# Layer openings of a two-layer diffusion backbone: the first two FFN tiles by token halves, with the splits moved between engines

## What is computed

```python
hx = modulate(rms_norm(x, norm1_g[l]), sh1x, sc1x)        # h * (1 + scale) + shift
x = x + g1x * mixer(hx)
x = x + g2x * swiglu(modulate(rms_norm(x, norm2_g[l]), sh2x, sc2x), ffn_w1[l], ffn_w3[l], ffn_w2[l])
def swiglu(h, w1, w3, w2):
    return (jax.nn.silu(h @ w1) * (h @ w3)) @ w2
```

## Time and profile before

| | us |
|---|---|
| median of three runs | 1555.65 (1554.92 to 1555.9) |
| the profiled execution | 1555.58 |
| its span, first to last instruction | 1553.8 |
| TensorE busy | 1489.6 (96%) |
| VectorE, ScalarE, GpSimd busy | 998.7, 699.8, 661.8 |

### The profile page before, as it was taken

How to read it: one execution, slowest core, us unless ns; L and a number is a source line. 1 busy time by engine, 2 the same in 40 slices (tenths; PEclk the granted TensorE clock), 3 DMA queues, 4 the chain that set the end, 5 groups by cost and what they waited for, 6 DMA issues and landing times.

```text
span 1553.8 us, 26593 instructions
## 1 busy us (share of the span) xinstructions
PE 1489.6 (96%) x10378; PEld 1271.7 (82%) x10378; DVE 998.7 (64%) x1480; ACT 699.8 (45%) x1211; POOL 661.8 (43%) x449
## 2 busy tenths in 40 slices
PE   6999999899899999999999999999999999999997
PEld 3888864479798889999899998855568998998997
DVE  5898877669586867667475455767623655455465
ACT  4745335562733324324243544245537354444355
POOL 0031036412655425444344333355646665556462
PEclk9999999999999999999999999999999999999999
DMA  9632110054124333354343111200012324224222
GB/s 376 217 117 80 43 42 0 3 199 152 58 99 159 109 119 127 116 181 154 120 159 113 61 63 55 68 28 1 1 55 70 129 77 134 70 93 131 89 95 82
DMA packets 51676, 157.07 MB, mean 101 GB/s; under 512 B 5568, under 2 KB 13120, under 8 KB 50016
## 3 DMA queue, kind: packets, MB, share of 16 engines
q1 hardware_dynamic: 51120, 155.17, 29.2%
q0 software_dynamic: 432, 0.20, 0.1%
HBM read 153.38 MB, written 2.10 MB: 100 GB/s over the span
## 4 chain that ended last, share of the span: by engine, by line
PE 63%; DVE 13%; issue 6%; ACT 5%; DMA 3%; POOL 2%; DVEq 0%; SPq 0%; ACTq 0%; POOLq 0%
PE psum L3332 23%; PE psum L3359 16%; PE psum L2745 9%; PE psum L3013 3%; DMA adr_late<-adat_dram 3%; DVE product L1831 3%; PE psum L2981 1%; PE psum L3304 1%; ACT bf L1568 1%; ACT fhi L1553 1%; PE psum L2912 1%; DVE psum L2414 1%; PE psum L2818 1%; DVE mx L1986 1%; POOL fraw L1118 1%
## 5 line engine op out<-in xcount | busy, mean ns | idle before, releaser
L1132 POOL TENSOR_TENSOR flow<-fraw,fhi 128x512 fp32r<-128x512 f32 x176 | 245.6, 1419 | 78.7 <-ACT fhi L1553 72.3
L1553 ACT ACTIVATE fhi<-fraw 128x512 fp32r<-128x512 f32 (+1 forms) x272 | 163.8, 614 | 212.6 <-POOL fraw L1118 114.3
L3359 PE MATMUL psum<-gated,fhi 128*128 128x512 f32 (+1 forms) x1032 | 255.0, 356 | 2.7 <-DVE gated L2393 2.7
L2745 PE MATMUL psum<-act,whi 128*128 128x512 f32 (+1 forms) x1008 | 215.5, 332 | 0.0
L1138 POOL TENSOR_TENSOR flow<-fraw,fhi 128x512 fp32r<-128x512 f32 (+1 forms) x96 | 124.7, 1316 | 198.3 <-ACT fhi L1553 197.8
L3332 PE MATMUL psum<-thi,fhi 128*128 128x384 f32 (+1 forms) x608 | 188.9, 311 | 7.4 <-ACT staged L1593 7.4
L3359 PEld LDWEIGHTS psum<-gated,fhi 128*128 128x128 f32 x1032 | 170.1, 189 | 31.5 <-DVE gated L2393 3.1
L3332 PE MATMUL psum<-tlo,fhi 128*128 128x384 f32 (+1 forms) x608 | 187.9, 309 | 0.0
L2745 PEld LDWEIGHTS psum<-act,whi 128*128 128x128 f32 x1008 | 154.0, 189 | 20.4 <-issue 1.8
L2460 DVE SCALAR_TENSOR_TENSOR xT<-psum,mod,xT 128x512 f32<-128x512 f32 (+1 forms) x141 | 87.8, 656 | 114.5 <-PE psum L3359 114.5
L3359 PE MATMUL psum<-gated,flow 128*128 128x512 f32 (+1 forms) x516 | 155.0, 356 | 0.0
(11 more groups left out here) (281 smaller groups left out, 3303.3 us busy)
## 6 DMA issues: line engine op xcount, KB each, us to landing
fraw<-weights_dram SPq DMA_DIRECT2D x88, 512.0 KB, 3.5
adr_late<-adat_dram SPq DMA_DIRECT2D x55, 512.0 KB, 4.3
raw<-weights_dram SPq DMA_DIRECT2D x44, 512.0 KB, 3.4
fraw<-weights_dram SPq DMA_DIRECT2D x64, 256.0 KB, 2.8
adr<-adat_dram SPq DMA_DIRECT2D x25, 512.0 KB, 4.6
ada_w<-ada_dram SPq DMA_DIRECT2D x8, 1024.0 KB, 12.8
fraw<-weights_dram SPq DMA_DIRECT2D x32, 192.0 KB, 2.5
xT<-x_in_dram SPq DMA_DIRECT2D x3, 1024.0 KB, 16.8
```

Of the source, the lines that this page charges most:

```text
L1132: nc.gpsimd.tensor_tensor(low_piece(L, j, x), weight_piece(L, j, x), high_piece(L, j, x).bitcast(F32), ALU.subtract).then_inc(sem("f_lo"), 1)
L1553: A(high_piece(L, j, x)[:, 0:cols], source, ACT.Copy).then_inc(sem("f_hi"), 1)
L2745: last = MM(out_[:, o:o + t1 - t0], w_, a_[:, t0:t1], start=k == order[0] and j == 0, stop=k == order[-1] and j == 2)
L3359: last = MM(ps, w_, a_[:, t0:t1], start=k == 0 and i == 0, stop=k == nk - 1 and i == 2)
```

## The change

1. **Order of the opening.** Tiles 0 and 1 are taken together: tile 0 with half 0, tile 1 with half 0, tile 0 with half 1, tile 1 with half 1 (`plain_half`). Tile 2 follows as before.
2. **Inputs.** VectorE scales and multiplies by the modulation in one operation (`token_scaled`, now a scalar_tensor_tensor) and adds the shift in a second one in place (`token_shifted`, a tensor_scalar on SBUF). ScalarE only makes the high part. GpSimd still makes the low part, for both layers. The low parts of weight pair 1 move from GpSimd to VectorE (`plain_low`).
3. **Mean of half 1.** One product on a completed sum instead of two; VectorE adds the last square (`end_add(L, 1, 2)`).
4. **Input sums.** T1 and T3 are made ahead of `plain_product(1)`, T2 and T4 behind it. Of the four low-part steps two go to GpSimd and two stay on VectorE, in the passes of the first two w2 pairs.
5. **Modulations.** One more tile in layer 0's output blocks; tiles 27 to 31 get buffers of their own and stand in the opening; units have one tile instead of two up to tile 47, then three as before; w2 pairs take one more from tile 48 on.
6. **Copies of products.** In a unit's pass, ScalarE's copies of products 7 and 6 stand ahead of the high part of S3.
7. **Layer 1's slots.** Pair 2 has a slot of its own and is loaded when the output blocks are done.
8. **`mean_square` for layer 1's projection** moves into the second block.

Of the diff, the edits that place these steps (context lines left out):

```diff
...
-LATE_OUT = [1, 2, 2, 2, 2]
+LATE_OUT = [2, 2, 2, 2, 2]
-LATE_END = 3
-N_LATE_FFN = len(LATE) - LATE_RING - LATE_END
+N_LATE_PAIRS = N_GATE2
...
 def raw_slot(layer, j):
+    if layer == 1:
+        return j % 3
...
 def late_in_pairs():
-    out, i = [], len(LATE) - N_LATE_FFN
+    out, i = [], N_LATE_PAIRS
-            n = [1, 2, 1][p["t"]]
+            n = 0
-            n = 2 if i < N_BOTH else 3
+            n = 1 if i < N_BOTH else 3
-            n = int(p["m"] in (2, 4))
+            n = int(p["m"] in (2, 4)) + int(i >= N_BOTH)
...
-                    if j == 4 and L == 1 and w == 0:
+                    if j == 2 and L == 1 and w == 0:
-                    elif j == 2 or j == 5:
-                        sp.wait_ge(*raw_used(L, j - 2 if j == 2 else 2, w))
-                    elif j == 3:
-                        sp.wait_ge(*raw_used(L, 1, w))
-                    elif j >= 6:
+                    elif L == 0 and j in (2, 3):
+                        sp.wait_ge(*raw_used(0, j - 2, w))
+                    elif L == 0 and j >= 5 or L == 1 and j >= 3:
...
-                        for i in range(LATE_RING, LATE_RING + LATE_END):
+                        load_late(LATE_RING)
+                    if L == 0 and j == 1:
+                        for i in range(LATE_RING + 1, N_GATE2):
-                    if L == 0 and 1 <= j <= 3:
-                        load_late_of_pair(j - 1)
...
+                    if j == PLAIN:
+                        for k in range(POOL_FORMS):
+                            form_sums_low(L, k)
...
             def token_input(L, h, k):
-                act.wait_ge(*token_z(L, h, k))
-                if (h, k) == (0, 0):
-                    act.wait_ge(sem("s_modA"), 3 + 2 * L)
-                    act.wait_ge(sem("s_mod"), 7 + 2 * L)
-                row = bf[L][h][:, k, :]
-                for a, e, c in token_parts(L, h):
-                    r_ = row[:, a - HALF[L] * h:e - HALF[L] * h]
-                    last = A(r_, r_, ACT.Identity, scale=modA[:, 2 * L + 1, k, c:c + 1], bias=mod[:, L, 24 + k, c:c + 1])
-                last.then_inc(sem("f_h"), 1)
-                A(form_high(L, token_form(h, k), k % KH), row, ACT.Copy).then_inc(sem("f_h"), 1)
+                A(form_high(L, token_form(h, k), k % KH), bf[L][h][:, k, :], ACT.Copy).then_inc(sem("f_h"), 1)
             def form_sums_high(L, k):
...
-                for k in range(0, 2):
+                end_power(L, 1, 1)
+                for k in range(0, 4):
-                end_power(L, 1, 1)
-                for k in range(2, 5):
-                    token_input(L, 0, k)
+                piece_high(L, 1, "A11")
+                token_input(L, 0, 4)
-                for k in range(5, KT):
-                    token_input(L, 0, k)
+                token_input(L, 0, 5)
+                piece_high(L, 1, "A21")
+                token_input(L, 0, 6)
+                piece_high(L, 1, "A12")
+                token_input(L, 0, 7)
+                piece_high(L, 1, "A22")
-                    if k == 5:
-                        piece_high(L, 1, "A11")
             def next_input(m):
...
             def ffn(L):
-                piece_high(L, 1, "A12")
-                piece_high(L, 1, "A21")
-                piece_high(L, 1, "A22")
-                for x in PIECES["plain"]:
-                    piece_high(L, 2, x)
+                piece_high(L, 2, "A11")
+                piece_high(L, 2, "A12")
+                piece_high(L, 2, "A21")
+                piece_high(L, 2, "A22")
-                form_sums_high(L, 0)
-                form_sums_high(L, 1)
-                form_sums_high(L, 2)
-                form_sums_high(L, 3)
+                for k in range(POOL_FORMS):
+                    form_sums_high(L, k)
...
-                    next_high(L, j, "unit", "S3")
+                    if j == PLAIN:
+                        for k in range(POOL_FORMS, KH):
+                            form_sums_high(L, k)
+                        product_copied(L, p["n"], 6)
+                    next_high(L, j, "unit", "S3")
-                    if unit:
-                        product_copied(L, p["n"], 6)
...
-                TT(bf[L][h][:, k, :], xT[:, k, halves(L, h)], bank(h)[:, 0:HALF[L]], ALU.mult).then_inc(sem("f_z"), 1)
+                if (h, k) == (0, 0):
+                    dve.wait_ge(sem("s_modA"), 3 + 2 * L)
+                    dve.wait_ge(sem("s_mod"), 7 + 2 * L)
+                o = HALF[L] * h
+                for a, e, c in token_parts(L, h):
+                    last = STT(out=bf[L][h][:, k, a - o:e - o], in0=xT[:, k, a:e], scalar=modA[:, 2 * L + 1, k, c:c + 1],
+                               in1=bank(h)[:, a - o:e - o], op0=ALU.mult, op1=ALU.mult)
+                last.then_inc(sem("f_z"), 1)
+            def token_shifted(L, h, k):
+                dve.wait_ge(*token_z(L, h, k))
+                o = HALF[L] * h
+                for a, e, c in token_parts(L, h):
+                    x_ = bf[L][h][:, k, a - o:e - o]
+                    last = TS(x_, x_, mod[:, L, 24 + k, c:c + 1], None, ALU.add)
+                last.then_inc(sem("f_z"), 1)
+            def plain_low(L, x):
+                dve.wait_ge(*piece_high_done(L, 1, x))
+                TT(low_piece(L, 1, x), raw_piece(L, 1, x), high_piece(L, 1, x).bitcast(F32), ALU.subtract) \
+                    .then_inc(sem("f_bl"), 1)
             def form_difference(L, x, a_, b_):
-            def forms_summed(L):
+            def forms_summed(L, second):
-                dve.wait_ge(*token_high(L, 1, KT - 1))
-                form_difference(L, "T1", b12, b11)
-                form_difference(L, "T3", b22, b12)
-                dve.wait_ge(*form_sum(L, 1))
-                form_difference(L, "T2", b22, t1)
-                dve.wait_ge(*form_sum(L, 3))
-                form_difference(L, "T4", b21, t2)
+                if not second:
+                    dve.wait_ge(*token_h(L, 1, KT - 1))
+                    if L == 0:
+                        dve.wait_ge(sem("s_atd"), late_sums(N_GATE2))
+                    form_difference(L, "T1", b12, b11)
+                    form_difference(L, "T3", b22, b12)
+                else:
+                    dve.wait_ge(*form_sum(L, 1))
+                    form_difference(L, "T2", b22, t1)
+                    dve.wait_ge(*form_sum(L, 3))
+                    form_difference(L, "T4", b21, t2)
             def form_sums_low(L, k):
...
-                if L == 0:
-                    late_modulation(LATE_RING + 1)
+                end_residual(L, 1, 1)
+                token_scaled(L, 0, 0)
+                token_scaled(L, 0, 1)
+                token_shifted(L, 0, 0)
+                token_scaled(L, 0, 2)
+                token_shifted(L, 0, 1)
+                end_add(L, 1, 1)
+                token_scaled(L, 0, 3)
+                token_shifted(L, 0, 2)
+                token_scaled(L, 0, 4)
+                token_shifted(L, 0, 3)
+                end_residual(L, 1, 2)
+                token_scaled(L, 0, 5)
+                token_shifted(L, 0, 4)
+                token_scaled(L, 0, 6)
+                token_shifted(L, 0, 5)
+                end_add(L, 1, 2)
+                token_scaled(L, 0, 7)
+                token_shifted(L, 0, 6)
+                plain_low(L, "A11")
+                token_shifted(L, 0, 7)
+                plain_low(L, "A21")
+                plain_low(L, "A12")
+                plain_low(L, "A22")
+                token_scaled(L, 1, 0)
+                for k in range(1, KT):
+                    token_scaled(L, 1, k)
+                    token_shifted(L, 1, k - 1)
+                    if L == 0 and k in (1, 4):
+                        late_modulation(LATE_RING + 1 + k // 4)
+                token_shifted(L, 1, KT - 1)
-                    late_modulation(LATE_RING + 2)
-                end_residual(L, 1, 1)
-                for k in range(0, 4):
-                    token_scaled(L, 0, k)
-                end_add(L, 1, 1)
-                for k in range(4, KT):
-                    token_scaled(L, 0, k)
-                end_residual(L, 1, 2)
-                for k in range(KT):
-                    token_scaled(L, 1, k)
+                    late_modulation(LATE_RING + 3)
             def ffn(L):
-                late_in_pair(L, 0, False)
-                forms_summed(L)
-                late_in_pair(L, 1, False)
-                late_in_pair(L, 1, True)
+                if L == 0:
+                    late_modulation(LATE_RING + 4)
+                    late_modulation(LATE_RING + 5)
+                    late_bias(0, 40, 48, N_GATE2)
+                forms_summed(L, 0)
+                forms_summed(L, 1)
-                for k in range(KH):
-                    form_sums_low(L, k)
-                late_in_pair(L, 2, False)
-                if L == 0:
-                    late_bias(0, 40, 48, N_GATE2)
...
+                    if j < PLAIN + KH - POOL_FORMS:
+                        form_sums_low(L, j - PLAIN + POOL_FORMS)
...
```

(27 more changed lines are left out.)

85 lines of the change are left out of this document (50 added, 35 removed).

## The result

The changed kernel takes 1531.95 us (median of 4 runs, 1530.83 to 1534.32) against 1555.29 us of the kernel before (4 runs of the same chip, 1554.78 to 1555.90). The ratio is 0.9852, 95% interval 0.9835 to 0.9869: 23 us faster, where 17.8 were forecast. The profiled run took 1530.83 us, and its span is 1529.0 (before 1553.8).

A forecast was written before the change was run, and what follows sets the result against it. TensorE, busy 96% of the span, was taken as the bound, leaving some 64 us. Terms 0 + 3.1 + 2.0 + 6.5 + 4.6 + 1.9 - 0.3 = 17.8 us, off 1555.65, gave 1538 us; range 1524 to 1548.

The forecast's parts named there:

- Layer 0's opening: Layer 0's first two tiles: removed waits offset by late inputs in half 1; gain 0, bounds +11.0 and -3.0 us.
- turns: Layer 0's opening: VectorE's shifts and GpSimd's low parts hold each other off, about 2.1 us a tile in half 1.
- the clock's term: Layer 0's opening: 1.5 us added because two TensorE gaps of 2 to 3 us may lower its clock again.
- One sign: Layer 0's opening: first L3290 product near 398.4, with TensorE idle below 0.5 us.
- Rival A: Openings: turns cost nothing, inputs keep pace with TensorE; 11.0 and 3.2 us more gained, 1524 us; chance 0.17.
- Layer 1's opening: Layer 1's first two tiles: end at 1211.5 instead of 1214.6; gain 3.1 us, bounds 6.3 and 0.
- First w2 group: Layer 0's first w2 blocks: gating wait goes, a late add behind tile 33 remains; gain 2.0 us, bounds 4.8 and 0.
- Units of layer 0: Layer 0's units: one modulation tile each removes seven waits caused by VectorE; gain 6.5 us, bounds 7.5 and 3.
- Units of layer 1: Layer 1's units: copies ahead of S3's high part remove five waits; gain 4.6 us, bounds 5.9 and 2.
- Squares: Layer 1's norm: TensorE's wait for the squares goes; gain 1.9 us, lower bound 0.
- B: Units, w2 blocks, layer 1's opening: waits change their place and gains shrink or vanish; 1548 us; chance 0.15.
- C: Units, chiefly layer 1's: S3's low part comes late, 2 us each, 38 us in all; near 1576 us; chance 0.05.

The follow-up runs named there:

- e4: Changed kernel with two modulation tiles a unit in layer 0, as before, instead of one, until tile 48; 1539.52 us.
- e5: Changed kernel with the old order of the opening's halves in both layers: both halves of tile 0, then both of tile 1; 1546.53 us.
- e2: Changed kernel with the shift of the inputs as an own ScalarE operation in both layers, the scale still on VectorE; 1525.22 us, ratio to the kernel before 0.9805.
- e7: Changed kernel with the shift on ScalarE in layer 0 alone and modulation tile 32 swept beside the first two w2 blocks; 1525.12 us.
- e9: Changed kernel with tile 1's products between tile 0's in layer 0's half 1, tile 32 earlier, and later w2 passes' modulation tiles spread differently; 1528.35 us.
- e3: Changed kernel with ScalarE's old order in units: high part of S3 ahead of product 7's copy, S2 ahead of 6's; 1538.57 us.
- e8: Kernel before with only the new order of copies in units and layer 1's squares' products moved to the projection's second block; 1546.68 us.
- e6: Changed kernel with the two modulation tiles swept between the inputs of layer 0's half 1 moved behind the last input; 1531.46 us.
- e10: Changed kernel with the shift on ScalarE in layer 0 and modulation tiles placed as in e9, without interleaved products; 1523.18 us, ratio to the kernel before 0.9800.
- e11: As e10, with half 1's sweeps behind the inputs and all four low parts of the input sums on GpSimd; 1537.87 us.

## Why the prediction was right, and where its steps were off

**The total.** Forecast 1538, range 1524 to 1548, measured 1531.95: right in sign and inside the range, 5.5 us low in the gain. By the profiled pair, the six terms that gained were all sized too small, by 0.6 to 1.6 us each; one that I had left at nothing costs 1.1; and 1.3 us lie ahead of the stages that the change shortens and are scatter.

**Layer 0's opening** (forecast 0, measured 1.6). The mechanism, turns, held. The end of tile 1 was due at 444.3 with the clock's term and came at 441.5. The last low part was due at 433.3 and ended at 431.84. The earlier start of the measured timeline is no part of this, since it was used up by the mean (due at 392.75, at 392.61) and the last output block's end (due at 398.3, at 398.29). The cycle was put at 2.1 us and measured 1.87; the shift alone at 0.30 and measured 0.41, in two parts 0.45 and 0.54. What failed is the last 1.5 us, added for the clock: TensorE idled 2.56 us, and the granted clock stayed at 1.00; and in e4, where it did fall behind the same wait, the opening took 42.5 us as well, because the slower products only filled later waits. One sign was missed: the first product came at 398.95, with 0.66 us of idle time ahead of it and not under 0.5. With e5 and e2 the zero is seen to be a sum of large terms: the alternation is worth 9.0 us with these inputs, the shift on VectorE takes 6.2 back. Rival A (the turns cost nothing) would have had this opening near 34.7 us (398.4 to 433.1); with the shift on ScalarE it is 36.3, here 42.5.

**Layer 1's opening** (3.1, measured 3.7). Laid out at 26.1 us from the first product to tile 2, measured 25.6; the half inputs of 256 columns are short enough for the turns.

**First w2 group** (2.0, measured 3.2). The mechanism stood as written: the wait of 2.74 us at the first block is gone, and one of 1.19 stands near its end, for the add behind tile 33's transfer. It was put at about 2.3 us (wanted at 483.3, done at 485.6): a mis-sized term. e7 and e9 show the cause by taking it away.

**Units of layer 0** (6.5, bound 7.5, measured 8.1). All waits went, and e4 brings them back. The bound was too low: seven waits of 5.8 us cost 8.1, so a wait costs 0.3 us beyond its length here, where I took 0.25, and I kept 1 us back for successors that did not come. **The price of the spreading** is the step that was missing: I looked for what a second tile costs in a unit and not for what two tiles cost in the later w2 passes, 1.1 us.

**Units of layer 1** (4.6, measured 5.3). e3 gives the same number from above and e8 from below. The residual waits in the two longest were put at 0.65 us each; the trace of the changed kernel has 0.41 and 0.35:

```profile
1232.57 0.39 PE L3392 MATMUL psum<-bhi,fhi 128*128 128x256 f32 x1 [0.41 <-ACT staged L1611]
...
1403.32 0.38 PE L3392 MATMUL psum<-bhi,fhi 128*128 128x256 f32 x1 [0.35 <-ACT staged L1611]
```

**Squares** (1.9, measured 2.6 here and 2.1 in e8, in a stretch that scatters by 1.3): right.

**The other rivals.** B held in one place only, the w2 group, and there in part: 1.19 us of wait stand where 2.74 were. C did not come: of 38 units two waited for a low part of GpSimd, 0.7 us in all, both the first unit of a group; the other 36 had all they wanted from GpSimd in time, S3 too. That part 7 gives nothing, and what the one tile more in the output blocks costs, was not tried alone. The traces bear on the latter, which was put at 0.3 us: from the third output block to the first opening product, TensorE's waits for the mean and for that product left out, the kernel before takes 52.1 us, e8 too, and the changed one 53.0. In the changed kernel TensorE waits once there for a low part of the output weights on GpSimd:

```profile
384.12 0.59 PE L2881 MATMUL psum<-act,whi 128*128 128x384 f32 x2 [0.38 <-POOL wlo L1200]
```

In e4, e6, e7, e9 and e10 one such wait, at 376 to 377 us, is 1.2 to 1.3 us long; the kernel before and e8, without the tile, have none.

## What to carry to other kernels

An operation that takes turns with the engine that ends its chain, as VectorE's shift does here with GpSimd's low part, does not overlap with it: the chain then runs step by step, whatever the engines' busy shares say. Try that operation on an engine that takes no such turns, even where it takes longer there (0.80 us against 0.54 made this opening 6.2 us shorter). And when a stretch gets shorter, look at once at the next fixed point of the slowest list: two ways to save 2 to 4 us in this opening gave nothing, and the one that was tried again with one transfer, 40 us later, started earlier gave 3 us.

## What the runs showed of the hardware

TensorE's clock, as the granted clock of the stretch behind a wait: after idle times of 3.39 and 2.74 us in the kernel before it is 0.57 and 0.63 over the next 4 us, after 3.56 us in e5 0.50 over 8 us, and after 6.76 us in e11 0.50 over 4. After 2.56 us in the changed kernel, 2.57 in e3 and 2.42 in e9 it is 1.00. But after the same 2.56 us in e4 it is 0.50 over 3 us, and in e5 it is 0.50 over 6 us behind waits of 1.88 and 0.53 us. So the length of one wait does not decide it: the same four waits, 5.1 us in all within 9 us, left the clock at 1.00 in two kernels and lowered it in a third. What decides is open.

A run's first 345 us, in which these kernels differ by one modulation tile at most, took 345.2 to 347.6 us in the thirteen profiled runs, while stages of units (44 to 190 us) later in the kernel agree within 0.1 us between kernels that have them alike. A difference of 1 us is read from a stage, and not from the whole time.
